# Forget-gate pairs laid out by feature, gate/up pieces loaded early, and two remainders made by accumulating transfers

## The reference, cut to what matters

```python
proj = h @ w_in
fq, fk, fv, fgate, dq, dk, dv = jnp.split(proj, IN_SPLITS, axis=-1)
log_f = jax.nn.log_sigmoid(fgate + fox_forget_b)
c = jnp.cumsum(log_f, axis=1).transpose(0, 2, 1)
fox_o = causal_block_attention(to_heads(fq, 8), to_heads(fk, 8), to_heads(fv, 8), c)   # adds c[t] - c[s] to the logits
...
diff_o = rms_norm(a1 - lam * a2, subln_g) * (1.0 - lam_init)                            # 4 differential heads
return jnp.concatenate([fox_o, diff_o], axis=-1) @ w_out
```

## Time and profile before

| what | value |
|---|---|
| median of 3 runs | 992.79 us (992.57 to 992.89) |
| span of the profiled execution, first to last instruction | 990.5 us |
| TensorE busy | 986.0 us (100%) |
| VectorE busy | 711.5 us (72%) |
| ScalarE busy | 486.3 us (49%) |
| GpSimd busy | 213.1 us (22%) |
| granted TensorE clock | 9 tenths or more in all 40 slices |
| transfers | 178.53 MB, mean 180 GB/s |

### The profile page before, as it was taken

How to read it: one execution, slowest core, us unless ns; L and a number is a source line. 1 busy time by engine, 2 the same in 40 slices (tenths; PEclk the granted TensorE clock), 3 DMA queues, 4 the chain that set the end, 5 groups by cost and what they waited for, 6 DMA issues and landing times.

```text
span 990.5 us, 14542 instructions
## 1 busy us (share of the span) xinstructions
PE 986.0 (100%) x5302; PEld 835.5 (84%) x5302; DVE 711.5 (72%) x849; ACT 486.3 (49%) x621; POOL 213.1 (22%) x215
## 2 busy tenths in 40 slices
PE   9999999999999999999999999999999999999998
PEld 6888888888888888888888888888888888888887
DVE  6766666775788767676777998678875767667674
ACT  6534343664666543434545444365555445334342
POOL 3313232014100232323112600060000012223230
PEclk9999999999999999999999999999999999999999
DMA  9665656745425656565745625544536456556561
GB/s 316 224 212 169 212 169 214 253 131 190 129 85 170 209 173 210 171 205 177 247 154 174 204 94 200 188 145 147 168 121 220 130 184 230 172 178 201 179 210 42
DMA packets 121017, 178.53 MB, mean 180 GB/s; under 512 B 5760, under 2 KB 82112, under 8 KB 120848
## 3 DMA queue, kind: packets, MB, share of 16 engines
q1 hardware_dynamic: 120048, 174.86, 53.8%
q0 software_dynamic: 576, 1.39, 0.5%
q10 hardware_dynamic: 352, 1.73, 0.5%
HBM read 176.88 MB, written 2.64 MB: 181 GB/s over the span
## 4 chain that ended last, share of the span: by engine, by line
PE 99%; DMA 0%; SPq 0%; ACT 0%; issue 0%; DVE 0%
PE acc L662 11%; PE acc L666 10%; PE acc L665 10%; PE tp L863 10%; PE gu L863 10%; PE gu L868 5%; PE tp L868 5%; PE tp L662 4%; PE tp L666 4%; PE tp L665 4%; PE gu L662 3%; PE gu L665 3%; PE gu L666 3%; PE acc L1143 2%; PE acc L1146 1%; PE acc L1172 1%
## 5 line engine op out<-in xcount | busy, mean ns | idle before, releaser
L2002 DVE TENSOR_TENSOR wlo<-raw,whi 128x2048 fp32r<-128x2048 f32 x140 | 325.7, 2331 | 153.9 <-ACT whi L1363 152.4
L1363 ACT ACTIVATE whi<-raw 128x2048 fp32r<-128x2048 f32 x150 | 285.7, 1908 | 70.3 <-PE acc L666 22.7
L863 PE MATMUL tp<-act_in,whi 128*128 128x512 f32 x432 | 102.9, 390 | 0.0
L863 PE MATMUL gu<-act_in,whi 128*128 128x512 f32 x432 | 102.6, 390 | 0.0
L1899 POOL TENSOR_TENSOR tmp<-tmp 128x256 f32<-128x256 f32 x54 | 39.7, 736 | 275.8 <-DVE tmp L2123 275.8
L1901 POOL TENSOR_TENSOR sil<-sil,tmp 128x256 f32<-128x256 f32 x54 | 88.8, 1644 | 33.5 <-ACT sil L1434 33.5
L863 PEld LDWEIGHTS gu<-act_in,whi 128*128 128x128 f32 x432 | 80.9, 188 | 16.6
L662 PE MATMUL acc<-whi,hT_hi 128*128 128x512 f32 x240 | 94.0, 392 | 0.0
L665 PE MATMUL acc<-wlo,hT_hi 128*128 128x512 f32 x240 | 93.7, 390 | 0.0
L666 PE MATMUL acc<-whi,hT_lo 128*128 128x512 f32 x240 | 93.4, 389 | 0.0
L863 PEld LDWEIGHTS tp<-act_in,whi 128*128 128x128 f32 x432 | 79.8, 188 | 15.7
(11 more groups left out here) (379 smaller groups left out, 1845.8 us busy)
## 6 DMA issues: line engine op xcount, KB each, us to landing
raw<-in_w_in SPq DMA_DIRECT2D x96, 512.0 KB, 4.7
raw<-in_down SPq DMA_DIRECT2D x66, 512.0 KB, 4.1
raw<-in_gate SPq DMA_DIRECT2D x64, 512.0 KB, 4.4
raw<-in_up SPq DMA_DIRECT2D x64, 512.0 KB, 4.9
raw<-in_w_out SPq DMA_DIRECT2D x16, 512.0 KB, 4.7
raw<-in_w_branch_hg SPq DMA_DIRECT2D x8, 512.0 KB, 4.3
raw<-in_w_branch_attn SPq DMA_DIRECT2D x8, 512.0 KB, 4.8
post<-in_post_gains SPq DMA_DIRECT2D x3, 512.0 KB, 6.2
```

The source lines that it names most:

```text
L863: pe.matmul(banks[:, a, :], w_hi[:, i, a * P:(a + 1) * P], both, start=i == 0, stop=False)
L1363: act.activation(split_weights(k)[0], raw[:, k % RING, :], ACT.Copy).then_inc(hi_ready, 1)
L2002: dve.tensor_tensor(w_lo, raw[:, k % RING, :], w_hi.bitcast(F32), ALU.subtract).then_inc(lo_ready, 1)
```

## The change

It has these parts, all in the first block's mixer and the start of the second FFN.

1. q and k of a forget-gate pair lie together in one 128-row buffer each (64 rows a head), and a pair's scores use two 64-row products beside each other, as the differential pairs do. The decays are split into three bf16 parts by GpSimd (copy, subtract, copy, subtract, copy), written to DRAM and read back into 6 rows a head, three of them decays and three of them ones; four bf16 products of 6 rows add them.
2. The values step has v as the stationary operand (64 columns a head) and the transposed weights as the moving one, so the result comes by feature. VectorE spreads the reciprocals (`fox_reciprocals`) to 64 columns a head, TensorE transposes them along with the weights (eight transposes instead of six), and `output` is one multiplication. ScalarE rounds the result (`fox_hi`), VectorE subtracts (`fox_lo`). `fills(T_WOUT, ..., 2, 3)` is gone on all engines.
3. The rests of `N_WOUT + 2` and `N_WOUT + 3` (`ADDED`) are no longer made by VectorE. ScalarE writes the negated rounding into `wlo` (`negative`), and a GpSimd transfer adds the piece from DRAM onto it (`accum_op=ALU.add`), counted by `added_in`.
4. `N_FFN2` and `N_FFN2 + 1` are loaded into `proj` (`raw_place`), not into the ring, and may come once four pairs' values and the roundings three pieces back are done.
5. ScalarE's list gets `hi(N_WOUT + 2)` right behind the weights' copy of pair 4, `negative(N_WOUT + 2)` ahead of the exponentials of pair 6, and `hi(N_WOUT + 3)` ahead of those of pair 7. `FOX_BEHIND` has more tiles ahead of the values and fewer behind them. VectorE's `lo(N_FFN2 + 1)` is cut into quarters between the steps of `norms_between(1)`.

The core of the diff:

```diff
-FOX_BEHIND = {4: (1, 2), 5: (1, 2), 6: (1, 1), 7: (0, 0)}
+FOX_BEHIND = {4: (2, 1), 5: (2, 1), 6: (2, 0), 7: (0, 0)}
...
+        def raw_place(k):
+
+            if k in (N_FFN2, N_FFN2 + 1):
+                return proj[:, k - N_FFN2, DQ:DQ + PIECE]
+            return raw[:, k % RING, :]
+
+        ADDED = (N_WOUT + 2, N_WOUT + 3)
...
-                if k >= RING:
-                    sp.wait_ge(lo_ready, k - RING + 1 + 3 * r)
+                if k in (N_FFN2, N_FFN2 + 1):
+                    sp.wait_ge(pv_done, 4)
+                    sp.wait_ge(hi_ready, k - RING + 1)
+                elif k - RING in ADDED:
+                    sp.wait_ge(negated, ADDED.index(k - RING) + 1)
+                elif k >= RING:
+                    sp.wait_ge(lo_ready, lo_n(k - RING) + 3 * r)
...
+                if pair(p)[0] == 0:
+                    pe.wait_ge(exp_done, p + 1)
+                    for h in range(2):
+                        for n in range(3):
+                            to = (n + 1) % 3 * P
+                            pe.transpose(turned[:, h, to:to + P], e_sb[:, h, n * P:(n + 1) * P], idn)
+                    pe.wait_ge(rden_ready, p + 1)
+                    for t in range(TT):
+                        mm = pe.transpose(turned[:, t, 3 * P:4 * P], fox_rden(p)[:, (1 - t) * P:(2 - t) * P], idn)
+                    mm.then_inc(pT_full, 1)
+                    return
...
+                if kind == 0:
+                    at = [slice(64 * h, 64 * h + 64) for h in range(2)]
+                    v = [proj[:, t, FV + i * P:FV + (i + 1) * P] for t in range(TT)]
+                    o = fox_place(p)
+                    for h in range(2):
+                        pe.matmul(o[at[h], 0, :], v[0][:, at[h]], fox_pT[:, h, 0:P], start=True, stop=True,
+                                  skip_group_check=True)
+                    for h in range(2):
+                        pe.matmul(o[at[h], 1, :], v[0][:, at[h]], fox_pT[:, h, P:S], start=True, stop=False,
+                                  skip_group_check=True)
+                    for h in range(2):
+                        mm = pe.matmul(o[at[h], 1, :], v[1][:, at[h]], fox_pT[:, h, S:3 * P], start=False, stop=True,
+                                       skip_group_check=True)
+                    mm.then_inc(pv_done, 1)
+                    return
...
             half(N_WOUT + 1, 0, wout_banks(1), 1, 0, tiles=[2, 3], first_j=1)
-            pe.wait_ge(o_out, 8)
-            fills(T_WOUT, from_proj(MIX), 2, 3)
             half(N_WOUT + 1, 0, wout_banks(1), 1, 1, first_j=1)
-            filled(T_WOUT, 3)
-            for b in range(2):
-                half(N_WOUT + 2 + b, 0, wout_banks(b), 0, 0, first_j=1).then_inc(acc_bank, 1)
-            filled(T_WOUT, 4)
+            pe.wait_ge(fox_lo_ready, 3)
+            half(N_WOUT + 2, 0, wout_banks(0), 0, 0, tiles=[0, 1, 2], first_j=1)
+            pe.wait_ge(fox_lo_ready, 4)
+            half(N_WOUT + 2, 0, wout_banks(0), 0, 0, tiles=[3], first_j=1).then_inc(acc_bank, 1)
+            half(N_WOUT + 3, 0, wout_banks(1), 0, 0, first_j=1).then_inc(acc_bank, 1)
...
+            def negative(k):
+
+                act.activation(split_weights(k)[1], raw_place(k), ACT.Copy, scale=-1.0).then_inc(negated, 1)
...
                 for p in range(4, 8):
                     weights_out(p)
+                    if p == 4:
+                        next_hi(N_WIN, 0, 23)
                     if p < 6:
                         q_out(p + 2)
+                    if p == 5:
+                        negative(N_WOUT + 2)
+                    if p == 6:
+                        hi(N_WOUT + 3)
                     if p < 7:
                         exps(p + 1)
-                    if p == 4:
-                        next_hi(N_WIN, 0, 23)
+                    else:
+                        negative(N_WOUT + 3)
+                    fox_hi(p)
...
             norm("diff")
+            for n, k in enumerate(ADDED):
+                pool.wait_ge(negated, n + 1)
+                pool.dma_start(split_weights(k)[1].rearrange("p (k n) -> p k n", k=4),
+                               wout_d.rearrange("(k p) n -> p k n", p=P)[:, 0:4, n * BLK:(n + 1) * BLK],
+                               accum_op=ALU.add).then_inc(added_in[n], 16)
...
+            def fox_reciprocals(p):
 
                 n = 6 * (p % 2)
                 dve.wait_ge(exp_done, p + 1)
-                dve.reciprocal(rden[:, n:n + 4], den[:, :]).then_inc(rden_ready, 1)
+                link(dve.reciprocal(rden[:, n:n + 4], den[:, :]))
+                dve.tensor_copy(heads(fox_rden(p), 4), per(rden[:, n:n + 4], 64)).then_inc(rden_ready, 1)
```

More of the change, by code:

```diff
@@ L234, in build @@
         hi_ready, lo_ready, piece_used = sem("hi_ready"), sem("lo_ready"), sem("piece_used")
+        negated, added_in = sem("negated"), [sem(f"added_in{n}") for n in range(2)]
         row_product, row_copied, row_padded = sem("row_product"), sem("row_copied"), sem("row_padded")
@@ L287, in split_weights, with lo_n @@
             return whi[:, k % RING, :], wlo[:, k % RING, :]
+        def raw_place(k):
[3 more added lines that the diff above has]
+        ADDED = (N_WOUT + 2, N_WOUT + 3)
+        def lo_n(k):
+            return k + 1 - sum(a < k for a in ADDED)
         def slot_former(k):
@@ L984, in scores @@
                 for h in range(2):
-                    rows_used = AUG if kind == 0 and h == 0 else P
-                    if kind == 0:
-                        q, k = (a[h][0:rows_used, i, :] for a in (fox_q, fox_k))
-                    else:
-                        q, k = q_sb[:, h, :], k_sb[:, h, :]
-                    lt, el = late_half(p, h), early_half(p, h)
-                    alone = kind == 2
-                    pe.matmul(lt, q[:, P:S], k, start=alone or h == 0, stop=alone, skip_group_check=not alone)
-                    mm = pe.matmul(el, q[:, 0:P], k[:, 0:P], start=alone or h == 0, stop=alone, skip_group_check=not alone)
-                if kind == 0:
-                    both = mask16.rearrange("p (o n) -> p o n", o=1).to_broadcast([P, 2, P])
-                    pe.matmul(heads(late(p), 2)[:, :, P:S], id16[:, :], both, start=False, stop=True, skip_group_check=True)
-                    mm = pe.matmul(heads(early(p), 2), id16[:, :], both, start=False, stop=True, skip_group_check=True)
+                    q, k = q_sb[:, h, :], k_sb[:, h, :]
+                    pe.matmul(late_half(p, h), q[:, P:S], k, start=True, stop=True)
+                    mm = pe.matmul(early_half(p, h), q[:, 0:P], k[:, 0:P], start=True, stop=True)
                 mm.then_inc(scores_done, 1)
@@ L1725, in _ @@
             diff_and_fox()
-            hi(N_WOUT + 3)
-            fills(T_WOUT, 2, 3)
             hi(N_FFN2)
@@ L2010, in half_lo, with tiles_lo @@
                 if b:
+                    ins.then_inc(lo_ready, 1)
+            def tiles_lo(k, a, n):
+                dve.wait_ge(hi_ready, k + 1)
+                cut = slice(a * BLK, (a + n) * BLK)
+                w_hi, w_lo = (w[:, cut] for w in split_weights(k))
+                ins = dve.tensor_tensor(w_lo, raw_place(k)[:, cut], w_hi.bitcast(F32), ALU.subtract)
+                if a + n == 4:
                     ins.then_inc(lo_ready, 1)
@@ L2088, in norms_between @@
                     postnorm(m, 0)
-                fill_by_halves(u, 0)
+                fill_scaled(u, 0)
+                if m == 1:
+                    tiles_lo(n1 + 1, 2, 1)
+                fill_rest(u, 0)
+                if m == 1:
+                    tiles_lo(n1 + 1, 3, 1)
                 if m == 3:
@@ L2211, in k_out, with maxima @@
                        .then_inc(kT_ready, 1)
-            def late_maxima(p):
-                dve.wait_ge(scores_done, p + 1)
-                n = 4 * (p % 2)
-                dve.tensor_reduce(mx[:, n:n + 2], heads(late(p), 2), AX, ALU.max)
-            def maxima(p, late_found=False):
+            def maxima(p):
                 dve.wait_ge(scores_done, p + 1)
@@ L2250, in weights_out @@
                     return
-                dve.tensor_copy(pT_sb[:, 1, :], turned[:, 1, 0:3 * P]).then_inc(pT_d, 1)
-                if pair(p)[0] == 0 and p != 6:
-                    reciprocals(p)
+                to, n = (pT_sb, 3 * P) if pair(p)[0] else (fox_pT, 4 * P)
+                dve.tensor_copy(to[:, 1, 0:n], turned[:, 1, 0:n]).then_inc(pT_d, 1)
             def late_reciprocals(p):
```

192 lines of the change are left out of this document (105 added, 87 removed).

## The result

The changed kernel takes 1005.78 us (median of five executions, 1002.86 to 1006.13) against 992.79 for the kernel before (five executions here, 992.57 to 995.71). The ratio on record, which goes by all executions, is 1.011, with a 95% interval of 1.0094 to 1.0126; the two medians alone stand at 1.013. The forecast was 996.2, +3.4, with a range up to 1001.5. The direction was right, the size was not.

The account below looks back on a forecast made before the run. TensorE, 99% of the chain, was taken as the bound. Work -2.5 and pauses +0.9, +0.15, +2.7 gave +1.2; transfer +2.0 and late rest +0.2 made +3.4: 993.9, plus 2.3 from span to median, 996.2 us; range 992.3 to 1001.5.

Parts of the forecast that it names:

- The work of the pairs: TensorE's work in forget-gate pairs 4 to 7: weights' transposes, values, dropped result transposes and old gaps, -2.5 us in all.
- The scores: Scores of each forget-gate pair on TensorE: 1.5 us against 1.52 before, no change, with -0.2 to +0.3 a pair for the range.
- the transposes: Weights' transposes of each forget-gate pair, eight instead of six: 0.2 us more a pair, +0.8 in all.
- the late rest of the norms: Last quarter of the cut lo pass delays the second rest beyond TensorE's product at 316.51: +0.2 us.
- The values: Values step of pairs 4 to 7 as twelve half-width passes: 0.85 us, 0.49 less a pair, -1.96 in all.
- rival D: Values step: half tiles do not overlap with 128 moving columns, +1.96 us of work, 997 us; chance 0.05.
- The pauses: TensorE stands for ScalarE's exponentials ahead of the weights' transposes: 0.9 us at pair 6, 2.7 at pair 7.
- The transfer: Second accumulating transfer lands after 8.7 us where TensorE has 6.7, so it waits 2.0; bounds 0 and 8.3.
- Rival C: Accumulating transfer slow, 12 to 15 us: TensorE waits 5.3 to 8.3, 999.5 to 1002.5 us; chance 0.17.

Follow-up runs that it names:

- ring loads: Changed kernel without accumulating transfers, exponentials of pairs 6 and 7 first, and the two early gate/up loads put back into the ring: 990.96 us, ratio 0.9986.
- run 1: Changed kernel without the accumulating transfers and negated roundings, VectorE subtracting both remainders again: 998.11 us, ratio 1.0030.
- run 2: Changed kernel with only ScalarE's list reordered, exponentials of pairs 6 and 7 ahead of the roundings, transfers kept: 1001.53 us, ratio 1.0078.
- run 9: The changed kernel measured once more with nothing edited: 1002.19 us, ratio 1.0094.
- run 10: Changed kernel with exponentials of pairs 6 and 7 first and the 1 MB load held until the second transfer lands: 996.02 us, ratio 1.0032.

## Why the prediction was wrong

**The work of the pairs: right in sign, 0.5 us too large.** From the scores of pair 4 to the features of the second FFN, the kernel before takes 325.64 - 268.89 = 56.75 us and the one with ring loads, which has no listed wait there, 324.21 - 269.23 = 54.98: -1.77, where -2.5 + 0.2 = -2.3 was forecast. The scores came out at 1.45 (1.5 said), the transposes at 0.79 for eight against 0.58 for six, +0.21 a pair (+0.2), the late rest of the norms at +0.28 (+0.2). Ahead of pair 7's transposes TensorE's weight loads still stand 0.34 us for the exponentials and 0.21 for the reciprocals, which had been put at nothing. The values gave 1.34 - 1.01 = 0.33 a pair instead of 0.49: 0.65 of the sum. The half-width passes do run beside each other, so rival D falls; the price was scaled from one row of 96 columns and came out 0.15 low: the twelve passes take 0.81 instead of 0.70, and the forecast's own 0.70 + 0.1 + 0.1 had been taken as 0.85. In rival D, 0.85 a pair was let fall into the pauses, more than the 0.49 a pair that its own term holds.

**The pauses: right.** 0.9 and 2.7 were forecast, 0.74 and 2.86 measured, at the two places named, released by the exponentials; and the rounding of the last piece waits for TensorE as said (0.86 in its row). Runs 1 and 2 show the cause by taking it away (run 1 the first pause, run 2 both).

**The transfer: the mis-sized term.** "I take 8.7, nearer to the middle rows" is where it failed. 8.7 is what the transfer takes alone (8.3 to 8.6). The text had named the 1 MB load that the same semaphore frees, and then took a value that has no load in it. Beside it, and beside SyncE's next load, the transfer took 12.3 us, and TensorE waited 5.34 instead of 2.0. Rival C had the mechanism and the wait (5.3 to 8.3), with 0.17. It too had nothing for the clock. The doubling was within reach: the plain transfer was put at 5.8 and takes 5.6, of which 2.6 are movement at 410 GB/s; moving twice the bytes adds another 2.6, which makes 8.2, and the first load's 1 MB on the same engines, at the same rate, would make 10.8 by this estimate; the rest up to 12.3 may be the second load's, which no run separates. The Trainium skill (DMA: Bandwidth & Descriptors, "Rules for kernel authors") says that an accumulate reads its destination and then writes it; the trace agrees, with 205 GB/s with the adding and 410 without, though no view shows the reads themselves. The 6.15 us of movement that the forecast named for a plain 1 MB was not seen: the plain transfer took 5.6 us from issue to landing, with issue and completion in it.

**The clock: the missing term.** The sum treated a wait as worth its own length and put nothing beside it, without a reason. Behind both long waits TensorE worked at the 1.2 GHz level. From the scores of pair 4 to the second FFN the changed kernel takes 339.14 - 272.29 = 66.85, 10.1 more than before; with -1.77 of work and 8.94 of waits 2.9 us are left for the clock, and keeping TensorE busy took 1.36 and 1.3 us off the two stretches behind the waits (2.2 in the whole program).

**The start: 3.1 us that are not the change's.** They are in the profiled execution and in the median, and were not to be foreseen from one profile; but the median fell into the later group. The miss does not hang on it: with an early start 1002.19 was measured (run 9), outside the range too. Another 0.3 us come up between the first features and pair 4's scores in the changed kernel and in the one with ring loads (269.23 - 19.60 against 268.89 - 19.55). 0.10 of it is the slower step ahead of pair 4's 64-row scores. 0.15 lies in pair 0's weights' transposes, here in the run with ring loads:

```profile
238.97 0.64 PE L1039 MATMUL acc<-fixed,att_e 128*128 128x128 f32 x3
```

In the kernel before the same three take 0.49. Here one of their weight loads stands 0.17 us for VectorE, whose subtraction ahead of that pair's maxima took 2.53 us instead of 2.28. GpSimd, to whose splitting of the decays the forecast gave no cost, works beside it; whether that is the cause, no run shows.

The terms together, against the span: -1.8 work, +8.9 waits, +2.9 clock, +3.1 start, +0.3 ahead of pair 4: +13.4, and 13.5 were measured. Forecast were -2.3, +5.75, 0, 0, 0. The medians lie 13.0 apart: the forecast put 2.3 us between span and median, and in the changed kernel they lie 1.8 apart.

**What the change could have been.** One transfer or none, and the exponentials first: 991.0 us beside 992.4. The gain that the layout makes (1.5 us) is at the edge of what can be told here, and it is all there is.

## What to carry to other kernels

- In a list written out by hand, ask of each long pass put ahead of a short one who waits for the short one. Two roundings of 1.8 us ahead of the exponentials cost 3.6 us of the engine that sets the end, and swapping lines took both pauses away.
- When a semaphore starts a transfer that is on the path, look up what else the same semaphore starts, and what stands behind that in its queue. Price the transfer with both beside it, and count an accumulating one as twice its bytes.
- A long wait of TensorE can cost more than its length: here 8.2 us in two waits cost 11, the rest at half the clock behind them. Put a chance on that whenever a forecast has such a wait in it.

## What the runs showed of the hardware

- An accumulating transfer from DRAM of 1 MB, issued by GpSimd with rows of 2 KB, moves mostly at 202 to 208 GB/s with the DMA engines nine tenths busy or more; without the adding, 403 to 416. It lands in 8.3 to 8.6 us alone, in 11.6 to 12.3 beside two 1 MB loads issued 0.3 us before and 4.1 to 5.5 us behind it, and in 9.2 when issued 6.6 us behind another of its kind. The plain one lands in 5.6 alone and in 7.9 beside the two loads.
- With waits of TensorE of 2.86 to 6.49 us the granted clock fell to 0.50 in every profiled execution of the unfilled kernels, during the wait or within some 1.3 us behind it; with 0.31, 0.48 and 0.74 it did not. How long it stayed down differs between executions of one kernel: at the second wait of the changed kernel some 3 us in its first profile and over 6 in the second (2.3 of them still within the wait), and over 6 in run 10. In two of the ten executions of run 1 and two of the ten of run 10 the mean clock shows no loss at all (1.000).
- At the start of the late executions the products step by 0.43 us up to 12 us, though the clock column of the windows has 1.00 there. In that stretch the steps have to be read, not the column.
- The program has two starts, some 3 us apart. Before forecasts are compared with medians of a few executions, the first group of products tells which of the two a trace is from.
